# Stick-breaking attention: sums of log keeps added onto the logits in their PSUM banks

## The chip, the core and the metric

The kernel runs on one core of one Trainium2 chip. The metric is the device time of one execution in microseconds, lower is better, and the median of several runs is given. Times in this text are microseconds unless marked ns. TensorE multiplies matrices and writes its results to PSUM, eight banks of 128 partitions by 512 fp32 values; VectorE and ScalarE read them from there.

## What is computed

Two blocks of two layers each run over a sequence of 256 tokens of width 1024. Every layer is a feed-forward part, a mixer and another feed-forward part, each with norms. The mixer of the two layers of the second block holds stick-breaking attention, eight heads of 64 dimensions, beside a short convolution and a pooling. Cut to the attention:

```
z = einsum('bqhd,bkhd->bhqk', q_blk, kh) * scale          # logits
mask = k_pos[None, :] < q_pos[:, None]                    # strictly causal
log_keep = where(mask, log_sigmoid(-z), 0.0)
between = cumsum(log_keep, axis=3, reverse=True) - log_keep
a = where(mask, exp(log_sigmoid(z) + between), 0.0)
out = einsum('bhqk,bhkd->bhqd', a, vh)
```

Since log_sigmoid(z) is z + log_sigmoid(-z), the exponent is z plus the sum of log_keep from the key itself to the last key ahead of the query.

## The kernel before

The program is written out by engine. TensorE, ScalarE, VectorE, GpSimd and the DMA queue each have an instruction list of their own, in the order in which the code is written, and wait for each other's semaphores. `SUBLAYERS` is the order of the twelve parts: "ffn", "ret", "mla" and, twice, "stick", the mixer with stick-breaking attention.

All weights stream through three slots of 128 x 2048 values. For each slot ScalarE makes a rounded copy (`high`, `w_hi`), VectorE makes the rest (`low`, `w_lo`), and TensorE takes three products for every weight tile (`cols_of`, lines L400 to L402). The projection of a stick layer is ten slots (`N_STICK`), and the output projection four more. Most of a "stick" part is this work. The attention lies between its slots.

The heads go in four pairs, s = 0 to 3, with head g = 0 or 1 of a pair on partitions 0 to 63 or 64 to 127 of `s_k` and `s_q`. Keys are on the output's partitions and queries on its columns: columns 0 to 255 of a bank are the first 128 keys against all queries, columns 256 to 383 the second 128 keys against the second 128 queries. `mid[0]` and `mid[1]` are the two banks of `down[0]`, `mid[2]` and `mid[3]` those of `down[1]`. For each pair:

- `pair_logits(s)` on TensorE writes z of both heads to `mid[0]` and `mid[1]` (L731, L732) and raises `s_z`. These products are 64 rows deep, since a head has 64 dimensions.
- `pair_log(s)` on ScalarE makes log(1 + exp(-|z|)) in three activations, with a table load ahead of some.
- `pair_keep(s)` on VectorE adds max(z, 0) (L1524), multiplies by minus the mask (L1527) and raises `s_lk`: the log keeps `z_lk`.
- `pair_sums(s)` on TensorE waits for `s_lk` and writes z plus the sums to `mid[2]` and `mid[3]`. It makes the logits a second time (L749, L752) and adds onto them a product of the log keeps with a triangle of ones, `tri`, for the keys of the same tile (L750, L753), and with a matrix of ones for the second key tile's part in the first (L751). It raises `s_cs`.
- `pair_min(s)` on VectorE cuts at zero and adds the mask (L1512), `pair_exp(s)` on ScalarE is the exponential (L1131), `pair_out(s)` on TensorE the product with the values (L763, L764), and `pair_high` and `pair_low` store it.

TensorE's order is: half a slot, logits 0, a slot and a half, sums 0, logits 1, a slot, output 0, half a slot, sums 1, logits 2, half a slot, output 1, a slot, sums 2, logits 3, a slot, output 2, sums 3, the pooling's product, the first half of the down product of the output projection, a wait for the minimum of pair 3 (`second`), its second half, output 3, and the rest. ScalarE's order around pair 2 is: the copy of a projection's result, the rounding of a slot, the exponential of pair 2, the logarithm of pair 3. VectorE's at the end is: log keeps of pair 3, store of pair 2, convolution of the first channel tile (its last line is L1552), minimum of pair 3, convolution of the second.

Of the kernel before, what the change touches and what calls it, by code (L numbers as in the profile page):

```python
# [17 lines left out]
P = 128  # L18
S = 256
# [15 lines left out]
CAUSAL = 384  # L35
# [62 lines left out]
def build(nc, ins, out):  # L98
# [3 lines left out]
    with ctx:  # L102
# [78 lines left out]
        s_q, s_k = as_.take(4, S), as_.take(4, S)  # L181
# [4 lines left out]
        z_lk = as_.take(2, CAUSAL)  # L186
# [16 lines left out]
        down = [ps("down0", 1024), ps("down1", 1024)]  # L203
        bank6, bank7 = ps("bank6", 512), ps("bank7", 512)
        gemm_bank = [bank0, bank1]
        mid = [down[0][:, 0:512], down[0][:, 512:1024], down[1][:, 0:512], down[1][:, 512:1024]]
# [34 lines left out]
        s_cs, s_min, s_exp, s_out, s_hi, s_lo = (sem(n) for n in ("s_cs", "s_min", "s_exp", "s_out", "s_hi", "s_lo"))  # L241
# [14 lines left out]
        def wait(eng, s, value):  # L256

            if value > 0:
                eng.wait_ge(s, value)
# [126 lines left out]
        def _(pe):  # L386
            mm, tr = nc.tensor.matmul, nc.tensor.transpose
# [5 lines left out]
            def cols_of(n, bank, hi=h_hi, lo=h_lo, tiles=range(2)):  # L393

                r = n % RING
                for j in tiles:
                    o = bank[:, j * S:(j + 1) * S]
                    for k in range(KD):
                        c = k * SC + j * P
                        mm(o, w_hi[:, r, c:c + P], hi[:, k, :], start=(k == 0), stop=False)  # L400
                        mm(o, w_hi[:, r, c:c + P], lo[:, k, :], start=False, stop=False)  # L401
                        last = mm(o, w_lo[:, r, c:c + P], hi[:, k, :], start=False, stop=(k == KD - 1))  # L402
                return last
# [5 lines left out]
            def gemm_rows_into(n, o, t, k_tiles, width, c0, n_cols, hi, lo):  # L409

                r = n % RING
                for i, k in enumerate(k_tiles):
                    c = i * width + c0
                    ts = slice(t * P, (t + 1) * P)
                    first, end = i == 0, i == len(k_tiles) - 1
                    mm(o, hi[:, k, ts], w_hi[:, r, c:c + n_cols], start=first, stop=False)
                    mm(o, hi[:, k, ts], w_lo[:, r, c:c + n_cols], start=False, stop=False)
                    last = mm(o, lo[:, k, ts], w_hi[:, r, c:c + n_cols], start=False, stop=end)
                return last

            def rows_of(n, bank, t, hi=h_hi, lo=h_lo):
                return gemm_rows_into(n, bank[:, t * S:(t + 1) * S], t, range(KD), SC, 0, SC, hi, lo)
# [184 lines left out]
            for u, kind in enumerate(SUBLAYERS):  # L607
                b = first_slot[u]
                if kind == "ffn":
# [15 lines left out]
                    for j in range(2):  # L625
                        for t in range(T):
                            last = tr(bank6[:, j * S + t * P:j * S + (t + 1) * P], act[:, t * SC + j * P:t * SC + (j + 1) * P], ident)
# [16 lines left out]
                if kind == "ret":  # L644
                    mem = list(mem_heads(0, 0))
                    first_slots(u + 1, [(b + j, next_bank()) for j in range(2)])
                    for j in range(2, N_RET):
# [4 lines left out]
                        for half in range(2):  # L652
                            if j < 3 or j >= 10:
                                last = rows_of(b + j, bank, half)
                            else:
                                last = cols_of(b + j, bank, tiles=(half,))
# [13 lines left out]
                elif kind == "mla":  # L670
# [4 lines left out]
                    for t in range(T):  # L675
                        for k in range(3):
                            bank, kk = (bank6, k) if k < 2 else (bank7, 0)
                            last = tr(bank[:, kk * S + t * P:kk * S + (t + 1) * P], c_nat[:, t, k * P:(k + 1) * P], ident)
# [4 lines left out]
                    for t in range(T):  # L683
                        for c in range(2):
                            last = gemm_rows_into(b + 3, mid[2 * t + c][:, 0:half], t, range(2), 2 * half, c * half, half, c_hi, c_lo)
# [4 lines left out]
                    for t in range(T):  # L690
                        for c in range(3):
# [3 lines left out]
                            last = gemm_rows_into(b + 4, bank[:, 0:third], t, (2,), 3 * third, c * third, third, c_hi, c_lo)  # L695
# [4 lines left out]
                    for i in range(6):  # L700
# [7 lines left out]
                        for g in range(2):  # L708
                            h = 2 * (i % 3) + g
                            for t in range(T):  # L710
                                last = tr(bank[0:QKW, g * S + t * P:g * S + (t + 1) * P], src[:, t, h * QKW:(h + 1) * QKW], ident)
# [11 lines left out]
                else:  # L723
                    c0 = 4 * sticks

                    def logits(s, banks, start, stop):

                        for g in range(2):
                            o = 64 * g
                            k, q = s_k[o:o + 64, s, :], s_q[o:o + 64, s, :]  # L730
                            yield g, 0, mm(banks[g][:, 0:S], k[:, 0:P], q, start=start, stop=stop)  # L731
                            yield g, 1, mm(banks[g][:, S:CAUSAL], k[:, P:S], q[:, P:S], start=start, stop=stop)  # L732

                    def pair_logits(s):
                        for _, _, last in logits(s, mid[0:2], True, True):
                            pass
                        last.then_inc(s_z, 1)

                    def pair_sums(s):

                        pe.wait_ge(s_lk, c0 + s + 1)
                        wait(pe, s_min, c0 + s)
                        tri, ones = cst("tri"), cst("ones")
                        for g in range(2):
                            o = 64 * g
                            k, q = s_k[o:o + 64, s, :], s_q[o:o + 64, s, :]
                            lk = z_lk[:, g, :]
                            first, second = mid[2 + g][:, 0:S], mid[2 + g][:, S:CAUSAL]
                            mm(first, k[:, 0:P], q, start=True, stop=False)  # L749
                            mm(first, tri, lk[:, 0:S], start=False, stop=False)  # L750
                            mm(mid[2 + g][:, P:S], ones, lk[:, S:CAUSAL], start=False, stop=True)  # L751
                            mm(second, k[:, P:S], q[:, P:S], start=True, stop=False)  # L752
                            last = mm(second, tri, lk[:, S:CAUSAL], start=False, stop=True)  # L753
                        last.then_inc(s_cs, 1)

                    def pair_out(s):
# [48 lines left out]
                    for j in range(2):  # L805
                        last = mm(bank0[:, j * S:(j + 1) * S], pool_w[:, j, :], pool_e[:, j, :], start=True, stop=True)
# [30 lines left out]
        def _(sc):  # L837
# [153 lines left out]
            for u, kind in enumerate(SUBLAYERS):  # L991
                b = first_slot[u]
# [43 lines left out]
                else:  # L1036
# [79 lines left out]
                    else:  # L1116
                        c0 = 4 * sticks
# [19 lines left out]
                        def pair_log(s):  # L1137

                            sc.wait_ge(s_z, c0 + s + 1)
                            z = down[0][:, :].rearrange("p (a b) -> p a b", a=2)[:, :, 0:CAUSAL]  # L1140
                            if s:
                                sc.wait_ge(s_exp, c0 + s)
                            act_fn(z_abs, z, ACT.Abs).then_inc(s_abs, 1)
                            sc.wait_ge(s_abs, 3 * (c0 + s) + 1)
                            act_fn(z_abs, z_abs, ACT.Exp, scale=-1.0).then_inc(s_abs, 1)
                            sc.wait_ge(s_abs, 3 * (c0 + s) + 2)
                            wait(sc, s_lk, c0 + s)
                            act_fn(z_ln, z_abs, ACT.Ln, bias=1.0).then_inc(s_abs, 1)

                        pair_log(0)  # L1150
                        slot_out(4)
                        high(b + 7)
# [36 lines left out]
        def _(ve):  # L1189
# [137 lines left out]
            for u, kind in enumerate(SUBLAYERS):  # L1327
                b = first_slot[u]
# [46 lines left out]
                else:  # L1375
# [75 lines left out]
                    elif kind == "mla":  # L1451
                        low(b + 3)
                        ve.wait_ge(c_rs, 1)
                        for t in range(T):
                            v.scalar_tensor_tensor(c_nat[:, t, 0:QR], c_nat[:, t, 0:QR], stat[:, 24 + t:25 + t], c_gain[:, 0:QR], ALU.mult, ALU.mult)
                            last = v.scalar_tensor_tensor(c_nat[:, t, QR:QR + KVR], c_nat[:, t, QR:QR + KVR], stat[:, 26 + t:27 + t],
                                                          c_gain[:, QR:QR + KVR], ALU.mult, ALU.mult)
# [24 lines left out]
                        for t in range(T):  # L1482
                            q = q_nat[:, t, :].rearrange("p (h d) -> p h d", h=HEADS_M)
# [4 lines left out]
                        for t in range(T):  # L1488
                            k = k_nat[:, t, :].rearrange("p (h d) -> p h d", h=HEADS_M)
                            kv = kv_nat[:, t, :].rearrange("p (h d) -> p h d", h=HEADS_M)  # L1490
                            v.tensor_copy(k[:, :, 0:NOPE], kv[:, :, 0:NOPE])
                            last = v.tensor_copy(k[:, :, NOPE:QKW], kr[:, t:t + 1, :].broadcast_to([P, HEADS_M, ROPE]))
# [9 lines left out]
                    else:  # L1502
                        c0 = 4 * sticks
# [3 lines left out]
                        def pair_min(s):  # L1507

                            ve.wait_ge(s_cs, c0 + s + 1)
                            cs = down[1][:, :].rearrange("p (a b) -> p a b", a=2)  # L1510
                            for g in range(2):
                                last = v.scalar_tensor_tensor(z_abs[:, g, :], cs[:, g, 0:CAUSAL], 0.0, cst("addmask"), ALU.min, ALU.add)  # L1512
                            last.then_inc(s_min, 1)
# [5 lines left out]
                        def pair_keep(s):  # L1519

                            ve.wait_ge(s_abs, 3 * (c0 + s) + 3)
                            z = down[0][:, :].rearrange("p (a b) -> p a b", a=2)
                            for g in range(2):
                                last = v.scalar_tensor_tensor(z_ln[:, g, :], z[:, g, 0:CAUSAL], 0.0, z_ln[:, g, :], ALU.max, ALU.add)  # L1524
                            link(last)
                            for g in range(2):
                                last = v.tensor_tensor(z_lk[:, g, :], z_ln[:, g, :], cst("negmask"), ALU.mult)  # L1527
                            last.then_inc(s_lk, 1)
# [168 lines left out]
```

## Time and profile before

| | |
|---|---|
| median of 3 runs | 2057.86 us (2056.94 to 2059.09) |
| span of the profiled execution | 2058.1 us |
| TensorE busy | 1980.5 us, 96% |
| TensorE weight loads busy | 1832.0 us, 89% |
| VectorE busy | 1087.5 us, 53% |
| ScalarE busy | 957.1 us, 47% |
| GpSimd busy | 139.7 us, 7% |
| HBM read | 354.19 MB, 173 GB/s over the span |

The span is the time from the first to the last instruction of one execution taken by the hardware profiler. The times of the three runs are listed beside it, and the profiled execution has no other time than its span. Each row of a timeline is an instruction, or several of one line merged, with its start, its length, its engine and line; a name of tiles like `down<-big,const` says what is written and from what it is read, without buffer numbers (`big` holds all of the attention's tiles in SBUF, `const` the triangle and the ones). TensorE's products overlap, so the distance from one start to the next is what a product costs, not its length. PE is TensorE's product, PEld its weight load, DVE VectorE, ACT ScalarE.

### The profile page before, as it was taken

How to read it: one execution, taken by the hardware profiler on the slowest of the kernel's cores; microseconds unless marked ns; L12 is line 12 of the kernel's file. 1: busy time of each engine (PE TensorE's matmuls, PEld its weight loads, DVE VectorE, ACT ScalarE, POOL GpSimd, SP SyncE). 2: the span in 40 equal slices, each digit the busy share in tenths (PEclk: the TensorE clock that was granted, in tenths of full speed). 3: DMA queues.
4: the chain of work that ended last, by engine and by line, in shares of the span. 5: the costliest groups of instructions: out<-in, count | busy, mean ns of one | idle time of the engine just before them, and what ended most of it. 6: DMA issues, size and time to landing. Idle time of an engine off the chain costs nothing.

```text
span 2058.1 us, 32564 instructions
## 1 busy us (share of the span) xinstructions
PE 1980.5 (96%) x13724; PEld 1832.0 (89%) x13724; DVE 1087.5 (53%) x990; ACT 957.1 (47%) x1097; POOL 139.7 (7%) x149
## 2 busy tenths in 40 slices
PE   7999999999999998999999999999999999999998
PEld 6999899899899986899989998889998998988997
DVE  4644656644554456544564445554446445456444
ACT  5445554533543356533453346553445335555443
POOL 2500022000000000000000002000000000200000
PEclk9999999999999999999999999999999999999999
DMA  8655543555465542455555555355555554535552
GB/s 286 205 183 184 168 154 129 199 187 185 146 214 188 188 148 81 162 186 183 184 185 184 183 165 184 103 174 190 187 164 194 186 189 147 185 103 174 184 185 101
DMA packets 261987, 356.46 MB, mean 173 GB/s; under 512 B 8976, under 2 KB 230544, under 8 KB 261904
## 3 DMA queue, kind: packets, MB, share of 16 engines
q1 hardware_dynamic: 258304, 342.15, 50.4%
q0 software_dynamic: 3600, 13.11, 2.1%
q8 instruction: 63, 1.03, 0.2%
q14 instruction: 20, 0.16, 0.0%
HBM read 354.19 MB, written 1.05 MB: 173 GB/s over the span
## 4 chain that ended last, share of the span: by engine, by line
PE 87%; DVE 6%; issue 3%; ACT 3%; DMA 1%; POOL 0%; SPq 0%; DVEq 0%; POOLq 0%; ACTq 0%
PE down L473 24%; PE bank L400 17%; PE bank L402 17%; PE bank L401 17%; PE bank L447 2%; PE bank L513 2%; DVE upd L1234 2%; ACT junk L852 1%; PE bank L438 1%; PE bank L439 1%; DVE w_lo L1203 1%; DVE xn L1214 1%; DVE x L1240 1%; DMA raw<-in_ffn_w_gu 1%; PE down L749 0%
## 5 line engine op out<-in xcount | busy, mean ns | idle before, releaser
L1197 DVE TENSOR_TENSOR w_lo<-raw,w_hi 128x2048 fp32r<-128x2048 f32 x300 | 687.8, 2295 | 522.9 <-ACT w_hi L881 522.9
L400 PE MATMUL bank<-h_hi,w_hi 128*128 128x256 f32 x2944 | 835.6, 284 | 0.0
L401 PE MATMUL bank<-h_lo,w_hi 128*128 128x256 f32 x2944 | 833.0, 283 | 0.0
L402 PE MATMUL bank<-h_hi,w_lo 128*128 128x256 f32 x2944 | 833.0, 283 | 0.0
L881 ACT ACTIVATE w_hi<-raw 128x2048 fp32r<-128x2048 f32 x322 | 614.2, 1908 | 263.8 <-PE down L473 201.4
L400 PEld LDWEIGHTS bank<-h_hi,w_hi 128*128 128x128 f32 x2944 | 564.7, 192 | 6.4 <-issue 2.5
L401 PEld LDWEIGHTS bank<-h_lo,w_hi 128*128 128x128 f32 x2944 | 564.8, 192 | 2.5
L402 PEld LDWEIGHTS bank<-h_hi,w_lo 128*128 128x128 f32 x2944 | 564.8, 192 | 0.0
L473 PE MATMUL down<-w_hi,m_hi 128*128 128x512 f32 x832 | 267.2, 393 | 0.0
L473 PE MATMUL down<-w_lo,m_hi 128*128 128x512 f32 x832 | 264.7, 390 | 0.0
L473 PE MATMUL down<-w_hi,m_lo 128*128 128x512 f32 x832 | 264.4, 389 | 0.0
L473 PEld LDWEIGHTS down<-w_hi,m_lo 128*128 128x128 f32 x832 | 156.2, 188 | 33.2
L473 PEld LDWEIGHTS down<-w_lo,m_hi 128*128 128x128 f32 x832 | 156.3, 188 | 33.0
L1002 ACT ACTIVATE m_hi<-big 128x512 fp32r<-128x512 f32 x80 | 50.3, 629 | 287.8 <-DVE big L1336 287.8
L473 PEld LDWEIGHTS down<-w_hi,m_hi 128*128 128x128 f32 x832 | 151.2, 189 | 27.7 <-issue 1.4
L998 ACT ACTIVATE big<-bank 128x512 f32<-128x512 f32 x88 | 52.6, 598 | 250.2 <-PE bank L402 219.3
L1336 DVE TENSOR_TENSOR big<-bank,big 128x512 f32<-128x512 f32 x88 | 60.9, 692 | 144.6 <-PE bank L402 109.5
L1588 POOL TENSOR_TENSOR stat<-stat,const 128x1 f32<-128x1 f32 x24 | 14.4, 599 | 1506.7 <-ACT stat L863 1506.7
L438 PE MATMUL bank<-w_hi,h_hi 128*128 128x256 f32 x384 | 95.3, 286 | 12.5 <-issue 7.2
L439 PE MATMUL bank<-w_hi,h_lo 128*128 128x256 f32 x384 | 93.9, 282 | 0.0
L438 PEld LDWEIGHTS bank<-w_hi,h_hi 128*128 128x128 f32 x384 | 73.3, 191 | 16.7 <-issue 10.4
L513 PE MATMUL bank<-const,xn 128*128 128x128 f32 x208 | 36.9, 315 | 45.5 <-DVE xn L1214 45.4
(207 smaller groups left out, 1395.1 us busy)
## 6 DMA issues: line engine op xcount, KB each, us to landing
raw<-in_ffn_w_gu SPq DMA_DIRECT2D x88, 1024.0 KB, 5.1
raw<-in_ffn_w_down SPq DMA_DIRECT2D x88, 1024.0 KB, 4.9
raw<-in_ffn_w_gate SPq DMA_DIRECT2D x44, 1024.0 KB, 5.3
raw<-in_ffn_w_up SPq DMA_DIRECT2D x44, 1024.0 KB, 5.4
raw<-in_w_in SPq DMA_DIRECT2D x20, 1024.0 KB, 5.2
raw<-in_ret_w_in SPq DMA_DIRECT2D x13, 1024.0 KB, 5.7
raw<-in_w_o SPq DMA_DIRECT2D x8, 1024.0 KB, 5.0
raw<-in_w_out SPq DMA_DIRECT2D x8, 1024.0 KB, 4.9
```

Of the source, the lines that this page charges most:

```text
L400: mm(o, w_hi[:, r, c:c + P], hi[:, k, :], start=(k == 0), stop=False)
L401: mm(o, w_hi[:, r, c:c + P], lo[:, k, :], start=False, stop=False)
L402: last = mm(o, w_lo[:, r, c:c + P], hi[:, k, :], start=False, stop=(k == KD - 1))
L438: mm(o, hi[:, k, ts], w_hi[:, n % RING, c:c + SC], start=(k == 0), stop=False)
L439: mm(o, lo[:, k, ts], w_hi[:, n % RING, c:c + SC], start=False, stop=False)
L473: last = mm(down[t][:, c * 512:(c + 1) * 512], a[:, k0 + j, ts], w[:, r, j * D + c * 512:j * D + (c + 1) * 512], start=(first and j == 0 a ...
L513: last = tr((bank6, bank7)[c][:, k * P:(k + 1) * P], xn[:, t, (4 * c + k) * P:(4 * c + k + 1) * P], ident)
L881: act_fn(w_hi[:, r, :], raw[:, r, :], ACT.Copy).then_inc(hi_ready, 1)
L998: act_fn(silu_g, bank0[:, :], ACT.Silu).then_inc(silu_done, 1)
L1002: act_fn(m_hi[:, k0:k0 + 2, :], act.rearrange("p (a b) -> p a b", a=2), ACT.Copy).then_inc(act_hi_done, 1)
L1197: v.tensor_tensor(w_lo[:, r, :], raw[:, r, :], w_hi[:, r, :].bitcast(f32), ALU.subtract).then_inc(lo_ready, 1)
L1336: v.tensor_tensor(act, bank1[:, :], silu_g, ALU.mult).then_inc(prod_done, 1)
```

## The change

`pair_logits(s)` writes into `mid[2 * (s % 2) + g]`, so the pairs take turns between `down[0]` and `down[1]`, and the log keeps' products of `pair_sums(s)` are added onto the same banks. The logits are made once. ScalarE and VectorE read `down[s % 2]`. The wait for `s_min` moves from `pair_sums(s)`, for the minimum of pair s - 1, to `pair_logits(s)`, for that of pair s - 2.

```diff
-                    def logits(s, banks, start, stop):
-
+                    def pair_logits(s):
+
+                        wait(pe, s_min, c0 + s - 1)
                         for g in range(2):
                             o = 64 * g
                             k, q = s_k[o:o + 64, s, :], s_q[o:o + 64, s, :]
-                            yield g, 0, mm(banks[g][:, 0:S], k[:, 0:P], q, start=start, stop=stop)
-                            yield g, 1, mm(banks[g][:, S:CAUSAL], k[:, P:S], q[:, P:S], start=start, stop=stop)
-
-                    def pair_logits(s):
-                        for _, _, last in logits(s, mid[0:2], True, True):
-                            pass
+                            z = mid[2 * (s % 2) + g]
+                            mm(z[:, 0:S], k[:, 0:P], q, start=True, stop=True)
+                            last = mm(z[:, S:CAUSAL], k[:, P:S], q[:, P:S], start=False, stop=True, skip_group_check=True)
                         last.then_inc(s_z, 1)
 
                     def pair_sums(s):
 
                         pe.wait_ge(s_lk, c0 + s + 1)
-                        wait(pe, s_min, c0 + s)
                         tri, ones = cst("tri"), cst("ones")
                         for g in range(2):
-                            o = 64 * g
-                            k, q = s_k[o:o + 64, s, :], s_q[o:o + 64, s, :]
-                            lk = z_lk[:, g, :]
-                            first, second = mid[2 + g][:, 0:S], mid[2 + g][:, S:CAUSAL]
-                            mm(first, k[:, 0:P], q, start=True, stop=False)
-                            mm(first, tri, lk[:, 0:S], start=False, stop=False)
-                            mm(mid[2 + g][:, P:S], ones, lk[:, S:CAUSAL], start=False, stop=True)
-                            mm(second, k[:, P:S], q[:, P:S], start=True, stop=False)
-                            last = mm(second, tri, lk[:, S:CAUSAL], start=False, stop=True)
+                            lk, z = z_lk[:, g, :], mid[2 * (s % 2) + g]
+                            mm(z[:, 0:S], tri, lk[:, 0:S], start=False, stop=True, skip_group_check=True)
+                            mm(z[:, P:S], ones, lk[:, S:CAUSAL], start=False, stop=True, skip_group_check=True)
+                            last = mm(z[:, S:CAUSAL], tri, lk[:, S:CAUSAL], start=False, stop=True, skip_group_check=True)
                         last.then_inc(s_cs, 1)
...
                         def pair_log(s):
...
-                            z = down[0][:, :].rearrange("p (a b) -> p a b", a=2)[:, :, 0:CAUSAL]
+                            z = down[s % 2][:, :].rearrange("p (a b) -> p a b", a=2)[:, :, 0:CAUSAL]
...
                         def pair_min(s):
...
-                            cs = down[1][:, :].rearrange("p (a b) -> p a b", a=2)
+                            cs = down[s % 2][:, :].rearrange("p (a b) -> p a b", a=2)
...
                         def pair_keep(s):
...
-                            z = down[0][:, :].rearrange("p (a b) -> p a b", a=2)
+                            z = down[s % 2][:, :].rearrange("p (a b) -> p a b", a=2)
```

On TensorE, from the last projection product ahead of the sums of pair 0 to the first logits of pair 1, before (L402 is the projection, L749 to L753 the sums, L731 the logits):

```order
L402 MATMUL bank1<-h_hi,w_lo 128x256
L749 MATMUL down1<-big 128x256 [waits s_lk]
L750 MATMUL down1<-big,const 128x256
L751 MATMUL down1<-big,const 128x128
L752 MATMUL down1<-big 128x128
L753 MATMUL down1<-big,const 128x128
L749 MATMUL down1<-big 128x256
L750 MATMUL down1<-big,const 128x256
L751 MATMUL down1<-big,const 128x128
L752 MATMUL down1<-big 128x128
L753 MATMUL down1<-big,const 128x128
L731 MATMUL down0<-big 128x256
```

And of the changed kernel at the same place (L743 to L745 are the sums, L733 the logits):

```order
L402 MATMUL bank1<-h_hi,w_lo 128x256
L743 MATMUL down0<-big,const 128x256 [waits s_lk]
L744 MATMUL down0<-big,const 128x128
L745 MATMUL down0<-big,const 128x128
L743 MATMUL down0<-big,const 128x256
L744 MATMUL down0<-big,const 128x128
L745 MATMUL down0<-big,const 128x128
L733 MATMUL down1<-big 128x256
```

The four products from `big` alone are gone from between those with the constants, and the logits that follow go to the other pair of banks.

On TensorE around the sums of pair 3, before (L763 and L764 are the output of pair 2, L806 is the pooling):

```order
L763 MATMUL bank6<-big 64x256
L764 MATMUL bank6<-big 64x128
L749 MATMUL down1<-big 128x256 [waits s_min,s_lk]
L750 MATMUL down1<-big,const 128x256
...
L753 MATMUL down1<-big,const 128x128
L806 MATMUL bank0<-big,pool_w 128x256 [waits small_in,pool_d,evac]
```

And of the changed kernel (L755 and L756 are the output, L798 is the pooling):

```order
L755 MATMUL bank6<-big 64x256
L756 MATMUL bank6<-big 64x128
L743 MATMUL down1<-big,const 128x256 [waits s_lk]
L744 MATMUL down1<-big,const 128x128
L745 MATMUL down1<-big,const 128x128
...
L798 MATMUL bank0<-big,pool_w 128x256 [waits small_in,pool_d,evac]
```

Here the sums follow another attention product and not a projection; the wait for `s_min` is gone from their head.

## Rows read from the trace of the kernel before

**Rows 1.** The page, parts 1 and 4: busy time, and the chain that ended last.

```profile
PE 1980.5 (96%) x13724; PEld 1832.0 (89%) x13724; DVE 1087.5 (53%) x990; ACT 957.1 (47%) x1097; POOL 139.7 (7%) x149
...
PE 87%; DVE 6%; issue 3%; ACT 3%; DMA 1%; POOL 0%; SPq 0%; DVEq 0%; POOLq 0%; ACTq 0%
```

**Rows 2.** Groups by line and shape: busy us, mean ns, idle before.

```profile
L749 PE MATMUL down<-big 64*128 64x256 f32 x32 | 11.1, 428 | 0.9 <-DVE big L1527 0.9
...
L752 PE MATMUL down<-big 64*128 64x128 f32 x32 | 7.8, 322 | 0.0
```

**Rows 3.** Timeline of TensorE at pair 0's sums: start, length, instruction.

```profile
1277.76 0.28 PE L401 MATMUL bank<-h_lo,w_hi 128*128 128x256 f32 x1
1277.88 0.28 PE L402 MATMUL bank<-h_hi,w_lo 128*128 128x256 f32 x1
1278.09 0.70 PE L749 MATMUL down<-big 64*128 64x256 f32 x2
...
1278.71 0.30 PEld L750 LDWEIGHTS down<-big,const 128*128 128x128 f32 x2 [0.33 <-issue]
1278.72 0.70 PE L750 MATMUL down<-big,const 128*128 128x256 f32 x2
...
1279.04 0.38 PE L750 MATMUL down<-big,const 128*128 128x256 f32 x1
...
1279.25 0.38 PE L751 MATMUL down<-big,const 128*128 128x128 f32 x2
1279.57 0.49 PE L752 MATMUL down<-big 64*128 64x128 f32 x2
1279.98 0.49 PE L753 MATMUL down<-big,const 128*128 128x128 f32 x2
...
1282.71 0.71 PE L731 MATMUL down<-big 64*128 64x256 f32 x4
```

**Rows 4.** Timelines of VectorE and TensorE ahead of the sums of pairs 1 and 2.

```profile
1289.75 1.03 DVE L1527 TENSOR_TENSOR big<-big,const 128x384 f32<-128x384 f32 x2
...
1293.39 0.70 PE L749 MATMUL down<-big 64*128 64x256 f32 x2
...
1305.05 1.03 DVE L1527 TENSOR_TENSOR big<-big,const 128x384 f32<-128x384 f32 x2
...
1308.68 0.70 PE L749 MATMUL down<-big 64*128 64x256 f32 x2
```

**Rows 5.** Timeline of TensorE from the sums of pair 3.

```profile
1321.42 0.70 PE L749 MATMUL down<-big 64*128 64x256 f32 x2 [0.44 <-DVE big L1527]
...
1329.56 0.62 PE L473 MATMUL down<-w_hi,m_hi 128*128 128x512 f32 x2
```

**Rows 6.** Waits of TensorE over the span: us in total, times, longest.

```profile
PE down L749 <- DVE big L1527: 0.9, 2, 0.4
```

**Rows 7.** Timeline of ScalarE from the table load of pair 2.

```profile
1311.20 1.28 ACT L1131 ACT_TABLE_LOAD   x1
1314.47 0.85 ACT L1131 ACTIVATE big<-big 128x768 f32<-128x768 f32 x1 [1.98 <-DVE big L1512]
...
1317.12 1.28 ACT L1148 ACT_TABLE_LOAD   x1
1318.41 0.84 ACT L1148 ACTIVATE big<-big 128x768 f32<-128x768 f32 x1
```

**Rows 8.** Timeline of VectorE from the log keeps of pair 3.

```profile
1320.35 1.03 DVE L1527 TENSOR_TENSOR big<-big,const 128x384 f32<-128x384 f32 x2
...
1323.94 0.43 DVE L1552 TENSOR_TENSOR big<-big 128x256 f32<-128x256 f32 x1
1326.15 1.02 DVE L1512 SCALAR_TENSOR_TENSOR big<-down,const 128x384 f32<-128x384 f32 x2 [1.78 <-PE down L753]
```

**Rows 9.** Windows: length, busy of PE, PEld, DVE, ACT, POOL, PEclk, DMA share, GB/s.

```profile
1278.09:1282.71 4.62, 4.62 (x22) 3.13 (x21) 1.46 (x1) 3.68 (x3) 4.37 (x6) 1.00 0.31 115
...
1360.00:1365.00 5.00, 5.00 (x33) 4.95 (x32) 4.62 (x4) 2.48 (x3) 0.53 (x1) 0.70 0.86 247
```

## The prediction

> **What bounds the kernel now.** I read the shares of the page first, then the chain that ended last [rows 1]: TensorE is busy 96% of a span of 2058.1 us and holds 87% of the chain. Time taken off TensorE is therefore time off the kernel, unless a wait opens behind it. The lines of the change come next [rows 2]: L749 and L752, the logits made a second time, show 32 rows each. Two layers of four pairs with two heads would be 16, so each fp32 product is run in two passes.
>
> The timeline of pair 0's sums [rows 3] shows what they cost. The last product of the projection ahead starts at 1277.88, and these follow each other by 0.12, so its place ends at 1278.00. The first of the sums starts at 1278.09, and the logits of the next pair at 1282.71. Inside, the first head's products start at 1278.09 (64 rows deep), 1278.72, 1279.25 (128 deep), 1279.57 (64) and 1279.98 (128). The second pass of L750, 256 columns, stands alone between two passes of its own form: 1279.04 to 1279.25, 0.21. But L749 takes 0.63 and not 0.42, and L752, 128 columns in two passes of 0.105, takes 0.41 and not 0.21. Each change between 64 and 128 rows costs about 0.1 on either side: a weight load ahead of the product is not hidden there (the row of PEld has 0.33 of idle time put down to issue [rows 3]).
>
> Then the timeline ahead of the other pairs' sums. At pairs 1 and 2 VectorE has the log keeps ready at 1290.78 and 1306.08 (start and length of L1527), while TensorE arrives at 1293.39 and 1308.68: slack of 2.61 and 2.60 [rows 4]. At pair 3 it is the other way: TensorE idles 0.44 until VectorE's L1527 is done, so it was free at 1320.98 and starts at 1321.42 [rows 5]. The second layer does the same: two such waits, 0.9 in all [rows 6]. Only there does a chain of ScalarE and VectorE set the time.
>
> **What the change removes.** Of each pair's sums, the four products of L749 and L752. By the gaps they hold 2 x (0.63 + 0.41) = 2.08 us. The neighbours gain too, since no product 64 rows deep is left between them. What stays, per head, is two passes of 256 columns (0.42) and four of 128 (0.42), all 128 deep: 0.84, for two heads 1.68. The change of form at the exit, to the next pair's logits, stays: I add 0.10. So 1.78 in place of 1282.71 - 1278.00 = 4.71, a gain of 2.9. I take it for pairs 0, 1 and 2, whose sums all stand behind a projection. Lower bound 2.08, if the neighbours keep their unhidden loads.
>
> At pair 3 the sums follow the output product of pair 2, another form, so the change at the entry stays. They run from 1321.42 to where 0.63 + 0.53 + 0.32 + 0.41 + 0.42 = 2.31 for each of two heads leads, 4.62 in all. New: 1.68 + 0.1 = 1.8. Gain 2.8.
>
> The Trainium skill, "TensorEngine Tiling (Array Packing)", section Tiling Modes, says that a change of tiling mode drains the engine. The trace agrees with it at L750 (0.33 us of issue). By columns alone, with no such cost saved, 768 columns of a pair would be 3 x 0.42 = 1.28 us and not 2.9: that is the second rival.
>
> **What it adds.** No instruction. The logits go to the other pair of banks every time; ScalarE's absolute value and VectorE's reads have the same shapes, so cost nothing more. The wait for a freed bank moves from the sums (for the minimum of the pair before) to the logits (for that of two pairs before). VectorE's minimum comes ahead of its own log keeps in the queue, and the sums in between have waited for those already: it costs nothing. No transfer or weight conversion is moved.
>
> **Where a new wait comes.** ScalarE's exponential of pair 2 stands behind the copy and conversion that the end of the projection releases, and behind its table load: 1311.20 + 1.28 = 1312.48. It starts at 1314.47, when VectorE has the minimum [rows 7]. With sums 2.9 shorter the minimum is ready 2.9 earlier, but ScalarE is free only 1.98 earlier (12.49 against 14.47). From there on ScalarE and VectorE run one chain to the log keeps of pair 3, so those come 1.98 earlier: 1319.44. TensorE is there at 1320.98 - 2.9 = 1318.08. It now waits 1.36 instead of 0.44; 0.92 is given back. For pairs 1 and 2: at worst the same 1.98 against 2.9, from slacks of 2.6, leaves over 1.6: no wait. A log keep made beside GpSimd's pool work may take 0.7 longer and is still covered.
>
> The Trainium skill, "ScalarE: Activation LUTs", section What ACT_TABLE_LOAD costs, gives 1.28 us for a load and about 1.38 more of drain. The trace has the 1.28, and the next activation starts where it ends: 1317.12 + 1.28 = 1318.40, against 1318.41 [rows 7], so a drain behind the load isn't there. By the page the exponential could be only 0.6 earlier, the wait would take back 2.3 a layer and the sum would be 18.4 instead of 21.2.
>
> At the end of the stage the next thing late is the minimum of pair 3. VectorE works on the convolution until 1324.37 and takes the minimum at 1326.15 [rows 8]. Measured from the log keeps (1320.35 + 1.03 = 1321.38) it is free 2.99 later, while the shorter sums end 1.9 later: the minimum starts about 1.1 after the sums instead of at once. It covers itself: TensorE asks for it ahead of the second half of the down product, at 1329.56 [rows 5], 3.5 after the sums' end, and it takes 1.02 [rows 8]. Slack 2.4 shrinks to 1.3. Cost nothing.
>
> **Sum.** A layer: 3 x 2.9 + 2.8 - 0.92 = 10.6. Two layers: 21.2. The span of the profile was 2058.1, which is 0.2 above the median of 2057.86: forecast 2057.9 - 21.2 = 2036.7.
>
> **The clock.** The sums run at a granted clock of 1.00 [rows 9]. Behind the turn between sublayers it falls: 0.70 over 1360 to 1365, so 1.5 us of work lost. Later turns come at other moments now; one such fall more or less, or two, makes +-3.
>
> **Rivals.**
> 1. ScalarE keeps the old pace: if the exponentials could not start earlier at all (another wait than the minimum holds them), the log keeps come as now. Then pair 3 gives back all 2.9 of pair 2, and pair 1 waits 1290.78 - 1290.49 = 0.3: 8.7 - 2.9 - 0.3 + 2.8 = 8.3 a layer, 2041.3. For it: the chain is already last at pair 3. Against: ScalarE stands idle 1.98 at L1131, with VectorE's minimum as releaser.
> 2. Only the columns go, since the cost of the changes comes back as something else: 1.28 x 8 = 10.2, and the exponential can follow it all, so 2047.7. Against: all passes left are of one form, as the 0.21 of L750's second pass.
> 3. No change: TensorE's time comes back at the next turn because weights or transfers pace the stage. Against: within the layer TensorE waits for no weights, and its only waits are those above. Within 0.2% (4.1 us, about what these measurements can tell) it would stay at 2057.9.
> 4. Slower: TensorE's clock falls to its lower level (half) in the wait ahead of pair 3's sums, which grows from 0.44 to 1.36. Every microsecond of work then done at half speed adds one. From 10.6 us of such work a layer the gain is used up. If the 8.1 us from 1321.42 to 1329.56 [rows 5] and as much behind them went at half, it would be 16 a layer: 2057.9 - 21.2 + 32 = 2068.7. Against: that the fall behind a turn costs 1.5, after longer waits.
>
> **Chances.** Forecast 0.74, rival 1 0.09, rival 2 0.10, rival 3 0.04, rival 4 0.03. So faster by over 0.2% 0.93, within 0.2% 0.04, slower 0.03. The range: forecast with the falls of the clock and with no wait given back (-1.8) down to 2032; up through rival 1, and the 2.08 bound (8 x 2.08 = 16.6, less 2 x 0.1 given back, 2041.5), with a fall more: 2045. That leaves out rivals 2 to 4, 0.17.
>
> **What would show it.** In the new profile: 1.8 from the first sum to the next pair's logits at pairs 0 to 2, with no 64-deep product between; PEld without idle time there; TensorE idle about 1.4 ahead of pair 3's sums, with VectorE's log keeps as releaser; none ahead of pairs 1 and 2; ScalarE's exponential of pair 2 right behind its table load; VectorE's minimum of pair 3 behind the convolution. The prediction is wrong if the sums take over 2.5, if other sums wait, or if the turns grow.

## The result

The changed kernel takes 2035.05 us in the median of four runs (2033.9 to 2037.55), beside 2058.48 for the kernel before in four runs. The ratio is 0.9889, with a 95% interval of 0.9875 to 0.9903. The forecast of 2036.7 lay 1.7 above it. A second set of five runs gave 2038.00 against 2059.74, ratio 0.9901 (0.9885 to 0.9918): 21.7 less instead of 23.4.

The page of the changed kernel, parts 1 and 4, to be read beside [rows 1]:

```profile
PE 1951.4 (96%) x13660; PEld 1813.0 (89%) x13660; DVE 1088.2 (54%) x990; ACT 956.7 (47%) x1097; POOL 140.2 (7%) x149
...
PE 86%; DVE 6%; issue 3%; ACT 3%; DMA 1%; POOL 0%; SPq 0%; DVEq 0%; POOLq 0%; ACTq 0%
```

TensorE has 64 rows less, the 64 of L749 and L752, and holds the chain as before. VectorE and ScalarE have the same number of instructions as before.

The timeline of TensorE at pair 0's sums in the changed kernel answers to [rows 3] (L743 to L745 are the sums, L733 the next logits):

```profile
1272.05 0.28 PE L402 MATMUL bank<-h_hi,w_lo 128*128 128x256 f32 x1
1272.17 0.59 PE L743 MATMUL down<-big,const 128*128 128x256 f32 x2
1272.60 0.38 PE L744 MATMUL down<-big,const 128*128 128x128 f32 x2
1272.82 0.39 PE L745 MATMUL down<-big,const 128*128 128x128 f32 x2
1273.05 0.60 PE L743 MATMUL down<-big,const 128*128 128x256 f32 x2
1273.48 0.38 PE L744 MATMUL down<-big,const 128*128 128x128 f32 x2
1273.70 0.39 PE L745 MATMUL down<-big,const 128*128 128x128 f32 x2
1274.02 0.71 PE L733 MATMUL down<-big 64*128 64x256 f32 x4
```

The first sum starts 0.12 after the last projection product, with no gap between them, and L743 takes 0.43, L744 and L745 0.22. From 1272.17 to 1274.02 it is 1.85, where the kernel before has 4.71. Pairs 1 and 2 take 1.84 and 1.85.

The same at pair 3, which answers to [rows 5] (L798 is the pooling, L806 in the kernel before):

```profile
1307.90 0.70 PE L743 MATMUL down<-big,const 128*128 128x256 f32 x2 [1.33 <-DVE big L1519]
...
1309.76 1.03 PE L798 MATMUL bank<-big,pool_w 128*128 128x256 f32 x4
```

and, in the kernel before, the row that follows its sums of pair 3:

```profile
1325.95 1.03 PE L806 MATMUL bank<-big,pool_w 128*128 128x256 f32 x4
```

So these sums take 1.86 (1307.90 to 1309.76) where the kernel before has 4.53 (1321.42 to 1325.95). The wait ahead of them has grown from 0.44 to 1.33. Over the span, beside [rows 6]:

```profile
PE down L743 <- DVE big L1519: 2.7, 2, 1.3
```

ScalarE at pair 2, beside [rows 7]:

```profile
1299.65 1.28 ACT L1123 ACT_TABLE_LOAD   x1
1300.94 0.85 ACT L1123 ACTIVATE big<-big 128x768 f32<-128x768 f32 x1
```

The exponential has no idle time ahead of it any more: it starts 0.01 after its table load ends, instead of 1.98.

**One length for all kernels.** The ends of the attention stage can be marked the same way in each kernel: from the start of pair 0's logits on TensorE to the moment ScalarE takes up the first half of the finished down product. In the kernel before, the two rows are these:

```profile
1268.41 0.71 PE L731 MATMUL down<-big 64*128 64x256 f32 x4
...
1340.36 0.60 ACT L852 ACTIVATE junk<-down 128x512 bf16<-128x512 f32 x1 [4.86 <-PE down L473]
```

and in the changed kernel:

```profile
1262.58 0.71 PE L733 MATMUL down<-big 64*128 64x256 f32 x4
...
1324.18 0.60 ACT L844 ACTIVATE junk<-down 128x512 bf16<-128x512 f32 x1 [4.86 <-PE down L473]
```

That is 71.95 and 61.60, a difference of 10.35; in the second layer 71.97 and 61.60, 10.37. So the change is worth 20.7 us. The spans differ by 26.1, and 5.8 of that is there before the first product of the change is reached (1268.41 against 1262.58). That part is the clock's, as the last experiment section shows.

### The profile page after: what moved, and what is told of

It reads as the page before. It is cut to its first block, busy times and chain, and to the rows that moved or that the text cites. A ratio compares the mean times of both kernels' runs of the same rounds, so it can differ in the third digit from the quotient of the medians.

```text
span 2032.0 us, 32432 instructions
## 1 busy us (share of the span) xinstructions
PE 1951.4 (96%) x13660; PEld 1813.0 (89%) x13660; DVE 1088.2 (54%) x990; ACT 956.7 (47%) x1097; POOL 140.2 (7%) x149
## 3 DMA queue, kind: packets, MB, share of 16 engines
q8 instruction: 63, 1.03, 0.2%
## 4 chain that ended last, share of the span: by engine, by line
PE 86%; DVE 6%; issue 3%; ACT 3%; DMA 1%; POOL 0%; SPq 0%; DVEq 0%; POOLq 0%; ACTq 0%
PE down L473 24%; PE bank L400 17%; PE bank L402 17%; PE bank L401 17%; PE bank L447 2%; PE bank L513 2%; DVE upd L1226 2%; ACT junk L844 1%; PE bank L438 1%; DVE w_lo L1195 1%; PE bank L439 1%; DVE xn L1206 1%; DVE x L1232 1%; DMA raw<-in_ffn_w_gu 1%; DVE w_lo L1189 0%
## 5 line engine op out<-in xcount | busy, mean ns | idle before, releaser
L402 PE MATMUL bank<-h_hi,w_lo 128*128 128x256 f32 x2944 | 833.0, 283 | 0.0
L402 PEld LDWEIGHTS bank<-h_hi,w_lo 128*128 128x128 f32 x2944 | 564.8, 192 | 0.0
L1332 DVE TENSOR_TENSOR m_lo<-big,m_hi 128x512 fp32r<-128x512 f32 x80 | 55.3, 691 | 44.6 <-ACT m_hi L994 44.6
```

The source lines that it names most:

```text
L1332: v.tensor_tensor(m_lo[:, k0:k0 + 2, :], act.rearrange("p (a b) -> p a b", a=2), m_hi[:, k0:k0 + 2, :].bitcast(f32), ALU.subtract).then_in ...
```

## The experiments

The stage lengths of all kernels, from the two rows named above, in each layer. The ratio of each is to runs of the kernel before that were made beside it (median 2057.35 of 20 for grouped, slivers and banks only, 2059.74 of 9 for the changed kernel again and early logits):

| kernel | layer 1 | layer 2 | median us | ratio to before (95%) |
|---|---|---|---|---|
| before | 71.95 | 71.97 | 2058.48 | |
| changed | 61.60 | 61.60 | 2035.05 | 0.9889 (0.9875 to 0.9903) |
| logits grouped | 64.72 | 64.72 | 2046.88 | 0.9936 (0.9916 to 0.9956) |
| slivers | 68.62 | 68.63 | 2049.61 | 0.9960 (0.9950 to 0.9971) |
| banks only | 71.96 | 71.95 | 2058.02 | 1.0007 (0.9997 to 1.0017) |
| exponential first | 61.34 | 61.30 | 2036.87, one run | |
| changed, again | 61.57 | 61.61 | 2038.00 | 0.9901 (0.9885 to 0.9918) |
| early logits | 59.99 | 59.99 | 2031.04 | 0.9866 (0.9847 to 0.9885) |
| pooling first | 60.75 | 60.71 | 2031.10, one run | |

The table separates two things. The lengths of a stage repeat to 0.04 us between layers and between runs of the same kernel, so a tenth can be read from them; the medians do not repeat so closely.

### Columns or changes of form: the logits grouped

The kernel before, with the remade logits of both heads ahead of the six products with the constants:

```diff
-                            yield g, 1, mm(banks[g][:, S:CAUSAL], k[:, P:S], q[:, P:S], start=start, stop=stop)
+                            yield g, 1, mm(banks[g][:, S:CAUSAL], k[:, P:S], q[:, P:S], start=False, stop=stop, skip_group_check=True)
...
+                        for _ in logits(s, mid[2:4], True, True):
+                            pass
                         for g in range(2):
...
-                            mm(first, k[:, 0:P], q, start=True, stop=False)
-                            mm(first, tri, lk[:, 0:S], start=False, stop=False)
-                            mm(mid[2 + g][:, P:S], ones, lk[:, S:CAUSAL], start=False, stop=True)
-                            mm(second, k[:, P:S], q[:, P:S], start=True, stop=False)
-                            last = mm(second, tri, lk[:, S:CAUSAL], start=False, stop=True)
+                            lk, z = z_lk[:, g, :], mid[2 + g]
+                            mm(z[:, 0:S], tri, lk[:, 0:S], start=False, stop=True, skip_group_check=True)
+                            mm(z[:, P:S], ones, lk[:, S:CAUSAL], start=False, stop=True, skip_group_check=True)
+                            last = mm(z[:, S:CAUSAL], tri, lk[:, S:CAUSAL], start=False, stop=True, skip_group_check=True)
```

> The kernel before, with all logits made twice as before, but in the sums both heads' logits come first and then the six products with the constants. No column is removed; the changes of form between 64 and 128 rows fall from eight to two per pair, and the two heads' 64-deep products stand next to each other, as in the first logits (four of them in 0.86 us there). Theory (columns 1.28 us and changes of form 1.6 us per pair both count): sums take about 2.7 instead of 4.62, 2.0 less per pair, nothing given back at pair 3: 15.8 in all, 2042.7. If 64-deep products side by side gained nothing, 1.3 per pair, 2048. Rival (only columns count): nothing but the packing, 2053 to 2058.

TensorE's timeline of one pair's sums in this kernel (L731 and L732 are logits, first the remade ones and at the end the next pair's; L748 to L750 the products with the constants):

```profile
1280.66 0.71 PE L731 MATMUL down<-big 64*128 64x256 f32 x4
1281.19 0.40 PE L732 MATMUL down<-big 64*128 64x128 f32 x4
1281.52 0.70 PE L748 MATMUL down<-big,const 128*128 128x256 f32 x2
...
1283.47 0.71 PE L731 MATMUL down<-big 64*128 64x256 f32 x4
```

The same columns take 2.81 instead of 4.62. The stage is 7.23 shorter in each layer, 14.5 in all, of the 20.7 that the change itself brings, and no product has been removed. The wait ahead of pair 3 stays at 0.44. The expectation of 15.8 was 1.3 too high; "only columns count" (at most 5) is out. The medians differ by 10.5 only (2057.35 and 2046.88): three of the five runs had a mean granted clock of 0.990 or 0.991. At 0.995 the one run took 2042.1, where the kernel before has 2055.4 to 2056.8.

All eight 64-deep passes together cost 0.86 here, less than the 1.28 of their columns one after another. The two heads' products stand side by side on different rows, and an overlap of the two would explain it. So of the 1.81 that grouping takes off a pair, up to 0.42 can be this overlap, and the other 1.39 is left for six changes of form, 0.23 each.

### The changes of form alone: slivers

The changed kernel, with 64-deep products of 8 columns put back where the logits stood, into columns that nobody reads:

```diff
+                            o = 64 * g
+                            spare = lambda c: mm(z[:, c:c + 8], s_k[o:o + 64, s, 0:P], s_q[o:o + 64, s, 0:8],
+                                                 start=False, stop=True, skip_group_check=True)
+                            spare(CAUSAL)
                             mm(z[:, 0:S], tri, lk[:, 0:S], start=False, stop=True, skip_group_check=True)
                             mm(z[:, P:S], ones, lk[:, S:CAUSAL], start=False, stop=True, skip_group_check=True)
+                            spare(CAUSAL + 8)
```

> The changed kernel, with four 64-deep products of 8 columns put back per pair, where the 64-deep logits stood, into columns of the bank that nobody reads. They bring back all changes of form and almost no columns (32 of 768). Theory: 8 changes at 0.2 each and four slivers make 1.7 to 2.1 per pair, less the wait at pair 3 that closes (0.9 a layer): 11.6 to 15 us over the changed kernel, 2047 to 2050. Rival (only columns count): under 1 us over it, 2036.

TensorE at one pair's sums (L744 is a sliver, L747, L748 and L750 the sums, L733 the logits):

```profile
1275.94 0.39 PE L744 MATMUL down<-big 64*128 64x8 f32 x2
1276.25 0.70 PE L747 MATMUL down<-big,const 128*128 128x256 f32 x2
1276.79 0.38 PE L748 MATMUL down<-big,const 128*128 128x128 f32 x2
1277.10 0.38 PE L744 MATMUL down<-big 64*128 64x8 f32 x2
1277.42 0.49 PE L750 MATMUL down<-big,const 128*128 128x128 f32 x2
1277.84 0.39 PE L744 MATMUL down<-big 64*128 64x8 f32 x2
...
1279.73 0.71 PE L733 MATMUL down<-big 64*128 64x256 f32 x4
```

A product of 8 columns takes 0.31 from its start to the next, and its 128-deep neighbours are longer than in the changed kernel: L747 0.54 against 0.43, L748 0.31 against 0.22, L750 0.42 against 0.22. The sums are back at 3.79, and the stage is 7.02 longer than in the changed kernel, 14.0 in all, though only 32 of 768 columns came back. The rival of under 1 us is out. The wait ahead of pair 3 fell from 1.33 to 0.44 at the same time (0.9 in two waits), so the slivers cost (7.02 + 0.89) / 4 = 2.0 a pair. The difference of 3.33 a layer between this and the kernel before is what the other 736 columns of a pair cost, 0.83 a pair.

The 2.0 holds the eight changes of form and the four small products themselves, their weight loads included. A product of 8 columns and 128 rows, which would change no form, was not run, so the products' own share is not shown. That the changes cost by themselves is shown by the grouped logits, where every product is still there.

### The banks alone

The changed kernel, with logits made a second time over the first ones, in the same bank:

```diff
+                            k, q = s_k[o:o + 64, s, :], s_q[o:o + 64, s, :]
-                            mm(z[:, 0:S], tri, lk[:, 0:S], start=False, stop=True, skip_group_check=True)
+                            mm(z[:, 0:S], k[:, 0:P], q, start=True, stop=False)
+                            mm(z[:, 0:S], tri, lk[:, 0:S], start=False, stop=False)
...
+                            mm(z[:, S:CAUSAL], k[:, P:S], q[:, P:S], start=True, stop=False)
```

> The moved banks and waits alone: pairs take turns between the two pairs of banks, the wait for the minimum is at the logits, but the sums make the logits a second time, over the first ones in the same bank. Theory: the banks and the moved wait cost and gain nothing, 2058.5 within 0.2%, sums 4.62 per pair, wait ahead of pair 3 0.44. Rival (the alternating banks free the order of work): faster than before by some microseconds.

The stages last 71.96 and 71.95, as in the kernel before, and the ratio is 1.0007. The sums of pair 0 take 4.62, and the wait ahead of pair 3 is the old one (0.9 in two waits). The alternating banks and the moved wait cost and give nothing by themselves.

### The wait ahead of pair 3: three ways at it

First ScalarE's queue. The rounding of a slot goes behind the attention's activations, and VectorE's rest of it behind the log keeps:

```diff
                         slot_out(8)
-                        high(b + 11)
                         pair_exp(2)
                         pair_log(3)
+                        high(b + 11)
...
                         pair_min(2)
-                        low(b + 11)
                         pair_keep(3)
+                        low(b + 11)
```

> The changed kernel, with ScalarE's exponential of pair 2 and logarithm of pair 3 ahead of the rounding of the slot that stood before them (and VectorE's rest of that slot behind the log keeps of pair 3). Theory (the wait of 1.3 ahead of pair 3's sums comes from ScalarE's queue, 1.9 of rounding and the table load): the wait falls to about 0.4, since the minimum is now last; but VectorE reaches the minimum of pair 3 some 2.3 later, so TensorE waits 1 to 2 ahead of the second half of the down product. In all 0 to 2 us over the changed kernel. Rival (the wait comes from TensorE's own side or VectorE): it stays at 1.3.

TensorE at the sums of pair 3 and at the second half of the down product:

```profile
1310.54 0.70 PE L743 MATMUL down<-big,const 128*128 128x256 f32 x2 [0.43 <-DVE big L1519]
...
1316.50 0.74 PE L473 MATMUL down<-w_hi,m_hi 128*128 128x512 f32 x2 [0.30 <-DVE big L1504]
```

The wait fell by 0.9, to 0.43, as expected, and a new one of 0.30 opened behind it, for the minimum of pair 3. I had put that at 1 to 2, and the whole at 0 to 2 us over the changed kernel. That was missed: the stage is 0.3 shorter. The grown wait did come from ScalarE's queue; a single run can't tell 0.6 us in the time.

Then TensorE's side. The pooling's product goes ahead of the sums of pair 3:

```diff
-                    pair_sums(3)
                     pe.wait_ge(evac, evacs[0])
...
                     last.then_inc(pool_mm, 1)
+                    pair_sums(3)
                     pe.wait_ge(s_lo, c0 + 2)
```

> The changed kernel with the pooling's product, 0.6 us of TensorE, ahead of the sums of pair 3 instead of behind them. Theory (TensorE is idle there and waits for a chain that does not depend on it): the wait falls from 1.3 to about 0.7 a layer, the sums start where they did, and the kernel is 1.2 us faster. Rival (the chain is pushed back with TensorE's work): the sums start 0.6 later and nothing is gained.

The rows at the place (L797 is the pooling):

```profile
1307.06 1.13 PE L797 MATMUL bank<-big,pool_w 128*128 128x256 f32 x4
1308.46 0.70 PE L743 MATMUL down<-big,const 128*128 128x256 f32 x2 [0.27 <-DVE big L1519]
```

The wait is 0.27, where I expected about 0.7, and the stage 0.85 to 0.89 shorter, 1.7 in all and a little over the 1.2 that I expected. The chain did not move with TensorE: the sums start 45.33 behind the stage's first row (1263.13), as in the changed kernel (45.32).

Last the chain itself. The second pair of banks lets the logits of pair 3 be made a slot earlier, and the first half of its logarithm:

```diff
                     pair_out(1)
+                    pair_logits(3)
                     gemm_cols(b + 8, next_bank())
                     pair_sums(2)
-                    pair_logits(3)
...
                         pair_high(1)
+                        pair_log(3)
                         slot_out(8)
                         high(b + 11)
                         pair_exp(2)
-                        pair_log(3)
+                        pair_ln(3)
```

Here `pair_log(3)` ends after the first exponential and `pair_ln(3)` is the logarithm; the minimum of pair 2 is written to `z_ln`, which is free by then.

> The changed kernel with what its two pairs of banks allow: the logits of pair 3 are made a slot earlier, behind the output of pair 1, once the minimum of pair 1 has freed their banks. ScalarE does the absolute value and first exponential of pair 3 before the end of the next slot; pair 2's minimum goes to the log keeps' first buffer, so the two do not collide. Theory (the 1.3 us ahead of pair 3's sums are ScalarE's queue and chain: table load, exponential, absolute value, exponential, table load, logarithm): the chain is 1.7 shorter and the load off it, so TensorE's wait there is gone, 2.7 us over both layers, and one change of form per layer less, 0.2 each: about 3 under the changed kernel, 2032 to 2033. Rival (something else delays the log keeps of pair 3): the wait stays over 1 and the time is that of the changed kernel.

ScalarE in this kernel from the exponential of pair 2 (L1123), with its idle time:

```profile
1309.24 0.85 ACT L1123 ACTIVATE big<-big 128x768 f32<-128x768 f32 x1 [0.41 <-DVE big L1513]
1310.11 1.28 ACT L1148 ACT_TABLE_LOAD   x1
1311.40 0.85 ACT L1148 ACTIVATE big<-big 128x768 f32<-128x768 f32 x1
```

The exponential is followed at once by the table load of the logarithm, and waits for VectorE's minimum again and not for its own table. VectorE has the log keeps of pair 3 at 1313.34 + 1.03 = 1314.37, and the list of TensorE's waits has none at the sums any more. The stage is 1.61 shorter than in the changed kernel, 3.2 in all, as expected (about 3). The medians are 2031.04 and 2038.00 in runs of one chip. More than half of that difference of 7.0 is not from the edit: at equal mean granted clock, 0.993 and 0.994, the runs differ by 3.4 and 2.6. This version beats both kernels.

### The clock and the spread of the runs

Each run has a mean granted clock of TensorE. Sorted by it, the 20 runs of the kernel before that stand beside the first experiments, and the runs of the changed kernel, read:

| mean granted clock | before, us | changed, us |
|---|---|---|
| 0.996 | 2054.5 to 2056.0 (3 runs) | 2033.9 |
| 0.995 | 2055.4 to 2056.8 (7) | 2034.1 to 2038.2 (5) |
| 0.994 | 2057.9 to 2059.0 (3) | 2037.6 |
| 0.993 | 2058.2, 2059.5 | 2038.0 |
| 0.992 | 2059.6 to 2060.5 (3) | |
| 0.991 | 2061.1, 2061.1 | 2040.7 |

The changed kernel's column holds both of its sets. Between 0.996 and 0.991 a run is 6 to 7 us longer, for either kernel. At equal clock the change is worth 20 to 21. In the trace the loss lies behind turns between sublayers. Windows of the changed kernel, with the clock third from the end:

```profile
1335.00:1340.00 5.00, 3.98 (x31) 3.58 (x31) 4.50 (x7) 3.23 (x6) 0.66 (x1) 1.00 0.32 88
1340.00:1345.00 5.00, 2.54 (x19) 2.10 (x18) 3.89 (x6) 4.36 (x9) 1.66 (x3) 0.94 0.60 199
1345.00:1350.00 5.00, 5.00 (x33) 5.00 (x33) 3.34 (x3) 1.44 (x2) 0.00 (x0) 0.72 0.91 279
```

In the window in which the fall begins TensorE was busy 2.54 of 5 us, and in the next, at a mean of 0.72, all of the time. In windows of 25 us the profile of the kernel before has eight under full clock, and that of the changed kernel three ahead of its end: 1325 to 1350, 1525 to 1550 and 1825 to 1850. The kernel before had falls at 225 to 250, 775 to 800, 850 to 875 and 1225 to 1250, all in code that the change doesn't touch.

These four account for the 5.8 us that are there ahead of the stage. L513, a product of the norms that both kernels have, marks the stretches. From one norm to the next the kernel before takes 94.71 (749.25 to 843.96) where the changed kernel takes 92.59 (748.10 to 840.69), with the fall at 775 to 800 inside. The stretches with the other three falls are 1.52, 1.35 and 1.20 longer. Where neither has a fall they agree within 0.02, as from 555.06 to 749.25 (194.19) against 553.92 to 748.10 (194.18). The falls come and go from run to run: the second profile of the changed kernel has nine such windows where the first has three, and reaches its stage at 1267.27 instead of 1262.58.

## Why the prediction was right

- **TensorE sets the time.** Right. What was taken off it, less the grown wait, came off the stage.
- **2.9 for pairs 0 to 2.** 4.71 - 1.85 = 2.86. The form change at the entry is gone, as L743's start 0.12 behind the projection shows. The term for a head, 0.84, measured 0.88 (1272.17 to 1273.05): each product is 0.01 to 0.02 longer than columns alone.
- **2.8 at pair 3.** 4.53 against 1.86: 2.67. The text had added up the gaps of pair 0 for the old sums and came to 4.62. The pooling behind them is 128 deep too (L806 at 1325.95), so there is no change of form at the exit, and the last product took 0.33 and not 0.42. This term was 0.1 too high.
- **0.92 given back.** The waits are 1.33 and 0.44: 0.89. The order of events was the one worked out: ScalarE's table load ends, its exponential follows, and what is behind it gains less than TensorE does. The sum of 18.4, with 1.38 of drain behind the load, is out: the load ends at 1299.65 + 1.28 = 1300.93 and the exponential starts at 1300.94. The experiment with the exponential first, and the one with early logits, took the wait away from two sides. What ends the wait by the trace is VectorE's L1519, but its cause is two steps back.
- **Sum.** 10.6 a layer against 10.35, 21.2 against 20.7. The terms measured add to 3 x 2.86 + 2.67 - 0.89 = 10.36.
- **Moves at no cost.** Shown by the banks alone.
- **The rivals.** That only columns go (10.2) is out: 736 of the 768 columns make 3.33 x 2 = 6.7 of the 20.7, and the changes of form, with the least products that make them, 14.0. The prediction's own split, 1.28 of columns and 1.6 of changes a pair, was off: the runs give 0.83 and 2.0. A 64-deep product of 8 columns takes 0.31 already, so part of what was counted as the columns' cost is there whatever the columns. The sum does not depend on the split, since the prediction read it from the gaps of the old trace. ScalarE at the old pace (8.3 a layer) is out by 10.35, and no change and slower are out by the result. The clock was 1.00 over both stages in every profile here, so the longer wait ahead of pair 3 brought no fall. The turns did not grow either. TensorE's largest wait, for the norms, is in the kernel before and in the changed one:

```profile
PE bank L513 <- DVE xn L1214: 45.4, 23, 11.2
...
PE bank L513 <- DVE xn L1206: 45.6, 24, 11.3
```

- **Log keeps of pair 1.** This was nearer than the text said. It allowed 0.7 for GpSimd beside it; on the timeline of VectorE and GpSimd in the changed kernel L1519 took 2.16 for both heads, where it took 1.03 in [rows 4]. The shorter sums moved it into GpSimd's pool work, which in the kernel before had ended at 1287.92 + 1.30 = 1289.22, ahead of L1527 at 1289.75 (the first row is of the kernel before, the others of the changed one):

```profile
1287.92 1.30 POOL L1666 TENSOR_TENSOR big<-big 128x512 f32<-128x512 f32 x1
...
1280.85 1.28 POOL L1657 TENSOR_TENSOR big<-big,const 128x512 f32<-128x512 f32 x1
...
1281.95 2.16 DVE L1519 TENSOR_TENSOR big<-big,const 128x384 f32<-128x384 f32 x2
...
1282.21 1.49 POOL L1658 TENSOR_TENSOR big<-big 128x512 f32<-128x512 f32 x1
```

It ends at 1284.11 and TensorE arrives at 1284.61. The slack of 2.61 is down to 0.50. The cover held, but the term was 1.13 and not 0.7; the other 0.98 of the loss is near the 0.92 by which the chain was to gain less than TensorE.

- **The minimum of pair 3.** VectorE took it at 1310.58, 0.8 behind the end of the sums, where the text had 1.1. TensorE didn't wait for it.
- **The rest, 23.4 instead of 20.7.** The text left +-3 for falls of the clock. The second set, 21.7, is nearer to the stage lengths. That the median came within 1.7 of the forecast is in part luck with the clock: the stage lengths, 0.5 from the forecast, are the better test. Which share of either median is clock can't be settled by windows alone; the comparison at equal clock is as far as it goes.

## What to carry to other kernels

Count the changes of tile form on TensorE before the columns. Here a product 64 rows deep between products 128 deep cost 0.3 us even at 8 columns, and 0.5 with what it cost its neighbours; grouping such products gave 14.5 us of the 20.7 that removing them gave. And where an engine is freed ahead of a chain through two others, look for what those do between the release and their next step: here a table load set how much of the gain could pass. Where the time of a whole run moves by 0.3% with its clock, as here, a small change is better read from a stage between two marks that every version has.

## What was not expected of the hardware

- The stage of 60 to 72 us repeated to 0.04 us between layers and between runs of one kernel, at a clock of 1.00, while whole runs spread over 6 to 7 us with the mean granted clock (0.996 to 0.991).
- VectorE's multiply of 128 x 384 fp32 from SBUF took 2.16 for two beside GpSimd's work (L1657 and L1658) and 1.03 without it.
